# The last head pair's attention spread over sixteen gate tiles, both merge gates taken ahead of both projections, and narrower waits at three joints

## The reference, cut to what matters

```python
h = rmsnorm(x); proj = h @ w_in      # q, ff, fb, i, ga, u, v, gb, ma, mb: 1024 columns each
y_a = rmsnorm_per_head(gla_forward(q, ff, i) + gla_backward(q, fb, i)) * silu(ga)   # 8 heads
y_b = gelu(u) * mix(layernorm(gelu(v)), w_s, b_s) * silu(gb)                          # 8 groups
merged = sigmoid(ma) * (y_a @ w_proj_a) + sigmoid(mb) * (y_b @ w_proj_b)
x = x + merged @ w_out
# second block: shift, scale, gate = split(silu(c) @ ada_w + ada_b), for c and for the context's c
# h = modulate(x, ...), hc = modulate(ctx, ...), then attention mixers
```

## Time and profile before

| what | value |
|---|---|
| median of 3 runs | 1622.14 us (1621.85 to 1622.33) |
| profiled execution, own time | 1623.66 us |
| its span in the trace | 1621.8 us |
| PE busy | 1530.3 us, 94% of the span |
| DVE, ACT, POOL busy | 709.6, 654.7, 537.2 us (44, 40, 33%) |
| mean granted PE clock | 0.979 of full |
| DMA | 122.71 MB, mean 76 GB/s |

### The profile page before, as it was taken

How to read it: one execution, slowest core, us unless ns; L and a number is a source line. 1 busy time by engine, 2 the same in 40 slices (tenths; PEclk the granted TensorE clock), 3 DMA queues, 4 the chain that set the end, 5 groups by cost and what they waited for, 6 DMA issues and landing times.

```text
span 1621.8 us, 21829 instructions
## 1 busy us (share of the span) xinstructions
PE 1530.3 (94%) x8872; PEld 1240.7 (76%) x8872; DVE 709.6 (44%) x1302; ACT 654.7 (40%) x1069; POOL 537.2 (33%) x472
## 2 busy tenths in 40 slices
PE   6999999999888979999899999999998999999997
PEld 5788897888777868877688898666787876666676
DVE  3237267274386311100267412777514435444423
ACT  6233243332323422222442132777624425555652
POOL 3333332333133464444542232333522240111221
PEclk9999999999999989999999999999998999999999
DMA  5533324224111135344321120200021120000011
GB/s 183 166 107 104 104 79 130 78 79 136 47 53 52 54 103 183 129 132 154 117 78 53 53 67 21 72 21 21 13 68 53 52 65 11 11 20 27 27 53 52
DMA packets 129314, 122.71 MB, mean 76 GB/s; under 512 B 11348, under 2 KB 125152, under 8 KB 129216
## 3 DMA queue, kind: packets, MB, share of 16 engines
q1 hardware_dynamic: 128960, 121.26, 23.8%
q10 hardware_dynamic: 256, 0.07, 0.0%
HBM read 116.87 MB, written 2.10 MB: 73 GB/s over the span
## 4 chain that ended last, share of the span: by engine, by line
PE 82%; DVE 10%; ACT 4%; POOL 2%; issue 2%; DMA 1%; ACTq 0%; DVEq 0%; SPq 0%
PE ps L2012 10%; PE ps L2013 9%; PE ps L2014 9%; PE ps L2473 4%; PE ps L2494 3%; PE ps L2321 3%; PE ps L2483 3%; PE ps L2312 2%; PE ps L2219 2%; PE ps L2058 2%; PE ps L2218 2%; PE ps L2220 2%; PE ps L2086 2%; PE ps L2474 2%; PE ps L2004 2%
## 5 line engine op out<-in xcount | busy, mean ns | idle before, releaser
L1136 POOL TENSOR_TENSOR w_lo<-raw,w_hi 128x512 fp32r<-128x512 f32 x320 | 421.6, 1350 | 798.7 <-ACT w_hi L651 740.4
L2012 PE MATMUL ps<-h_hi,w_hi 128*128 128x512 f32 x632 | 255.1, 404 | 12.1 <-POOL yb_lo L1159 8.7
L2013 PE MATMUL ps<-h_lo,w_hi 128*128 128x512 f32 x632 | 248.0, 392 | 0.0
L2014 PE MATMUL ps<-h_hi,w_lo 128*128 128x512 f32 x632 | 247.6, 392 | 0.0
L651 ACT ACTIVATE w_hi<-raw 128x2048 fp32r<-128x2048 f32 (+1 forms) x77 | 145.5, 1890 | 130.2 <-PE ps L2014 32.7
L2012 PEld LDWEIGHTS ps<-h_hi,w_hi 128*128 128x128 f32 x632 | 120.4, 190 | 44.7 <-issue 18.8
L2014 PEld LDWEIGHTS ps<-h_hi,w_lo 128*128 128x128 f32 x632 | 119.7, 189 | 26.0
L2013 PEld LDWEIGHTS ps<-h_lo,w_hi 128*128 128x128 f32 x632 | 120.3, 190 | 23.2
L1901 DVE CUSTOM_DVE_ANT_0 prob_b<-ps,no_mask 128x768 f32<-128x768 f32 x64 | 61.0, 954 | 72.7 <-PE ps L2474 72.7
L1078 ACT ACTIVATE pT_b<-ps 128x512 f32<-128x512 f32 x96 | 52.1, 594 | 71.3 <-PE ps L2483 71.3
L2004 PE MATMUL ps<-w_hi,h_hi 128*128 128x256 f32 x256 | 73.7, 288 | 0.0
(11 more groups left out here) (444 smaller groups left out, 3361.0 us busy)
## 6 DMA issues: line engine op xcount, KB each, us to landing
raw<-in_w_in_dram SPq DMA_DIRECT2D x32, 1024.0 KB
raw<-in_ada_w_dram SPq DMA_DIRECT2D x24, 1024.0 KB
raw<-in_a_w_in_dram SPq DMA_DIRECT2D x10, 1024.0 KB
raw<-in_w_in_dram SPq DMA_DIRECT2D x16, 512.0 KB
raw<-in_b_w_in_dram SPq DMA_DIRECT2D x5, 1024.0 KB
raw<-in_w_proj_a_dram SPq DMA_DIRECT2D x4, 1024.0 KB
raw<-in_w_proj_b_dram SPq DMA_DIRECT2D x4, 1024.0 KB
raw<-in_w_out_dram SPq DMA_DIRECT2D x4, 1024.0 KB
```

Of the source, the lines that this page charges most:

```text
L1136: last = nc.gpsimd.tensor_tensor(w_lo[:, ph.w(s), p], raw[:, s % 2, p], w_hi[:, ph.w(s), p].bitcast(F32), ALU.subtract)
L2012: mm(ps[:, j, :], wh[:, k, c], xh[:, k, :], start=(k == 0), stop=False)
L2013: mm(ps[:, j, :], wh[:, k, c], xl[:, k, :], start=False, stop=False)
L2014: last = mm(ps[:, j, :], wl[:, k, c], xh[:, k, :], start=False, stop=(k == KT - 1))
```

## The change

Five edits:

1. `GATE_SLOT` spreads GLA slots 0 to 11 over all 16 gate tiles: tiles 2, 5, 8 and 11 have none.
2. The rounding of `y_a` leaves the gates phase. ACT does all 8 `ya_hi` at the start of the merge, behind the rounding of the second strip; POOL does `ya_lo` in two blocks of four, behind the second and the third strip's `w_lo`.
3. The merge takes ma, mb, ada, ada, pa, pb, so both gates come before both projections.
4. Waits: PE no longer waits for all of `ya_lo` and `yb_lo` ahead of the merge but tile by tile inside the first pa and pb tile. ACT's wait for `yb_lo` moves to the first mb. `ada_strip` in the heads phase waits only for the strip before the last one.
5. `c_tok` moves onto `ya_hi`'s place and its load stands behind the first w_out strip and waits only for the last pa tile.

```diff
-MERGE_STRIPS = ("ma", "pa", "ada", "ada", "mb", "pb")
+MERGE_STRIPS = ("ma", "mb", "ada", "ada", "pa", "pb")
+GATE_SLOT = (0, 1, None, 2, 3, None, 4, 5, None, 6, 7, None, 8, 9, 10, 11)
-        c_tok = at("c_tok", [P, NC, D], F32, r_vs)
+        c_tok = at("c_tok", [P, NC, D], F32, r_ya)
...
@@ SP
                     load(outs, it, s, [(k_of(raw, s % 2), w_out[:, :, (2 * it + s) * STRIP:(2 * it + s + 1) * STRIP])])
-            sp.wait_ge(s_mh, KT)
-            sp.wait_ge(s_ml, KT)
-            sp.dma_start(c_tok[:, :, :], ...).then_inc(s_in2, 16)
+                    if not (it or s):
+                        sp.wait_ge(s_proj, merge.t(merge.iters - 1, MERGE_STRIPS.index("pa")) + 2)
+                        sp.dma_start(c_tok[:, :, :], ...).then_inc(s_in2, 16)
@@ ACT, gates
-                    if tt <= 10:
-                        gla_act(g_last, tt)
+                    slot = GATE_SLOT[tt]
+                    if slot is not None:
+                        gla_act(g_last, slot)
-                    if tt >= 12:
-                        act.wait_ge(s_y, PAIRS + 1)
-                        for k in (2 * (tt - 12), 2 * (tt - 12) + 1):
-                            nc.scalar.activation(ya_hi[:, k, :], y_a[:, k, :], ACT.Copy).then_inc(s_yah, 1)
@@ ACT, merge
+                    if it == 0 and kind == "ma":
+                        act.wait_ge(s_y, PAIRS + 1)
+                        for k in range(KT):
+                            nc.scalar.activation(ya_hi[:, k, :], y_a[:, k, :], ACT.Copy).then_inc(s_yah, 1)
+                    if it == 0 and kind == "mb":
+                        act.wait_ge(s_ybl, GCH)
-            act.wait_ge(s_ybl, GCH)
@@ POOL, merge
-                for s in merge.split[1:]:
+                for x, s in enumerate(merge.split[1:]):
                     lo(merge, it, s)
+                    if it == 0 and x < 2:
+                        ya_low(*range(4 * x, 4 * x + 4))
@@ PE
-                if not (isinstance(a, int) and a < 1):
-                    pe.wait_ge(s_adaev, a)
+                free = a - 1 if ph is heads else a
+                if free > 0:
+                    pe.wait_ge(s_adaev, free)
...
-                    if tt <= 11:
-                        gla(PAIRS - 1, tt + 1)
+                    if GATE_SLOT[tt] is not None:
+                        gla(PAIRS - 1, GATE_SLOT[tt] + 1)
...
-            pe.wait_ge(s_yal, KT)
-            pe.wait_ge(s_ybl, GCH)
...
-                        project(merge, it, s, j, False, x_hi, x_lo)
+                        low = {"pa": (s_yal, 0), "pb": (s_ybl, 0)}.get(kind)
+                        project(merge, it, s, j, False, x_hi, x_lo, ready=None if it or j else low)
...
+                            if it == 0:
+                                pe.wait_ge(s_yb, GCH)
                             ada_strip(merge, it, MERGE_ADA[s, j], 7 - merge.j(MERGE_ADA[s, j]))
```

More of the change, by code:

```diff
@@ L572, in _ @@
                     load(outs, it, s, [(k_of(raw, s % 2), w_out[:, :, (2 * it + s) * STRIP:(2 * it + s + 1) * STRIP])])
-            sp.wait_ge(s_mh, KT)
-            sp.wait_ge(s_ml, KT)
-            sp.dma_start(c_tok[:, :, :], t["ctx_2"][0, :, :].rearrange("(n p) d -> p n d", p=P)).then_inc(s_in2, 16)
+                    if not (it or s):
+                        sp.wait_ge(s_proj, merge.t(merge.iters - 1, MERGE_STRIPS.index("pa")) + 2)
+                        sp.dma_start(c_tok[:, :, :], t["ctx_2"][0, :, :].rearrange("(n p) d -> p n d", p=P)).then_inc(s_in2, 16)
             sp.wait_ge(s_xt, 2 * KT)
@@ L817, in _ @@
                         nc.scalar.activation(tmp[:, 0, :], ps[:, 0, :], ACT.Square).then_inc(s_sigg, 1)
-                        gla_keys(g_last, tt)
+                        if slot is not None:
+                            gla_keys(g_last, slot)
                         hi(*((gates, (g + 1) // 2, (g + 1) % 2) if g + 1 < GCH else (merge, 0, 0)))
@@ L842, in merge_act @@
                             act.wait_ge(s_free, merge.t(it, s) + j - 1)
-                            nc.scalar.activation(tmp[:, x + j, :], ps[:, j, :], ACT.Sigmoid).then_inc(s_sigm, 1)
+                            nc.scalar.activation(tmp[:, 2 * x + j, :], ps[:, j, :], ACT.Sigmoid).then_inc(s_sigm, 1)
                         if (s, j) in MERGE_SUM:
@@ L857, in merged_hi @@
                     nc.scalar.activation(h_hi[:, k, :], merged[:, k, :], ACT.Copy).then_inc(s_mh, 1)
-            act.wait_ge(s_proj, merge.t(merge.iters - 1, merge.split[2]) + 2)
+            act.wait_ge(s_proj, merge.t(merge.iters - 1, merge.split[1]) + 2)
             merged_hi(*range(KT - 2))
@@ L1167, in _, with ya_low @@
                     split_y(g - 1)
[L1168 to L1171, removed]
             split_y(GCH - 1)
+            def ya_low(*tiles):
+                for k in tiles:
+                    pool.wait_ge(s_yah, k + 1)
+                    nc.gpsimd.tensor_tensor(ya_lo[:, k, :], y_a[:, k, :], ya_hi[:, k, :].bitcast(F32), ALU.subtract).then_inc(s_yal, 1)
             for it in range(0, merge.iters):
-                for s in merge.split[1:]:
+                for x, s in enumerate(merge.split[1:]):
                     lo(merge, it, s)
+                    if it == 0 and x < 2:
+                        ya_low(*range(4 * x, 4 * x + 4))
                 if it + 1 < merge.iters:
@@ L1519, in _ @@
                     tt = 2 * g + j
-                    gla_slot(PAIRS - 1, tt)
+                    if GATE_SLOT[tt] is not None:
+                        gla_slot(PAIRS - 1, GATE_SLOT[tt])
                     if tt == 0:
@@ L1548, in merge_dve @@
                         col = bass.ds(2 * it + j, 1)
-                        if x in (0, 2):
-                            dve.wait_ge(s_sigm, 4 * it + x + j + 1)
+                        if x < 2:
+                            dve.wait_ge(s_sigm, 4 * it + 2 * x + j + 1)
                             dve.wait_ge(s_free, merge.t(it, s) + j)
                             dve.sem_inc(s_free, 1)
-                        elif x == 1:
+                        elif x == 2:
                             dve.wait_ge(s_proj, merge.t(it, s) + j + 1)
```

## The result

| what | before | changed |
|---|---|---|
| median, first chip | 1622.24 us (1621.85 to 1622.64, 4 runs) | 1594.33 us (1591.09 to 1595.41, 4 runs) |
| ratio | | 0.9825, 95% interval 0.9808 to 0.9842 |
| profiled execution, own time | 1623.66 us | 1594.2 us |
| its span | 1621.8 us | 1592.4 us |

The forecast was 1589.5 us with a range from 1584.5 to 1599.0. The change is faster by 27.9 us by the medians and by 29.4 by the two spans, where 32.7 were forecast. The median lies in the stated range and 0.3 us above the narrower one, 1585 to 1594, that the prediction gave its own sum.

A forecast was written before the change was run, and what follows sets the result against it. PE, busy 94% of the span, was taken as the bound, its waits also lowering its clock. Heads 14.8, gates and merge 12.9 and context 5.0 sum to 32.7 us saved, giving 1589.5 us, range 1584.5 to 1599.

The forecast's parts named there:

- Heads, 14.8 us: Heads phase: the ada matmuls' four waits go, saving 3.55 us in each of three iterations and 4.15 in the first.
- Rival 2: Heads: the wait moves to DVE or a strip's load, 12 of 14.8 us stay, 1601.5 us; chance 0.05.
- Gates, wait before step 4: Gates phase: PE waits 4.5 us for DVE's doubling before GLA step 4, against 3.7 before, plus 1.4 of lower clock.
- Gates, the other waits: Gates phase: waits of 1.0 and 0.9 us for `w_lo`, 0.9 for a key copy, 3.1 before GLA step 8.
- the gain at steps 1 and 2: Early gates phase: no gain was forecast; the 2.5 us wait before GLA step 2 and its lower clock were to stay.
- The loss at step 8: Gates phase: 1.4 us lost to PE's lower clock behind the wait before GLA step 8.
- Merge, 1.85 - 1.0 = 0.85: Merge: its first tile gets 1.85 us shorter at a higher clock, less 1.0 us of waits in the first pa tile.
- Rival 3: Merge: each of its 16 `w_lo` comes late, at 3 us a strip costing 48 us, ending at 1637; chance 0.02.
- Context, 5.0 us: Context's transposes: the 5.92 us load wait goes; ACT's first copy comes 4.6 us earlier, plus 0.4 from the clock.
- Rival 1: Gates phase: DVE's doublings before GLA steps 4, 6 and 8 wait for POOL pieces, costing 8 us, 1597.5; chance 0.13.
- Rival 4: Heads, first merge tile, context: only the waits leave, clock gains shrink by 5 us, 1594.5 us; chance 0.09.
- The signs that the prediction named: Ada waits gone, merge some 27 us earlier, longest gates wait before GLA step 4, short pa wait, transposes directly behind out tile.

The follow-up runs named there:

- The experiment: Changed kernel with ACT's rounding of the third w_out strip moved behind the eight context copies to `xcT`: 1585.51 us, ratio 0.9763 to the kernel before.
- the version with early offsets: Changed kernel with DVE's eight one-time offset instructions moved from the start of gate group 1 into group 0: 1591.87 us, ratio 0.9781 to the kernel before.

## Why the prediction was right, and where it was off

- **Heads, 14.8 us: right.** The row of `k_sum` came 15.3 us earlier, and the steps next in line wait 0.22 where 0.3 was priced. Rival 2 had nothing. Alone it gave 13.2 by the medians and 13.9 by that row.
- **Gates, wait before step 4: the step that was mis-sized.** The forecast took the doubling's time behind the group's first tile from the old order, offsets included, and said 4.5 us; it measured 6.99. It took over the 2.17 us of the offsets without asking what POOL does beside them once PE, and with it the strip, comes earlier. The runs show 2.17 to 2.18 us with POOL behind, 5.3 to 6.3 with POOL beside; of the 4.15 us that they grew by, the work behind them, free of the strip, gave more than half back. (The prediction's own terms give 13.1 - 8.2 - 0.25 = 4.65 where it says 4.5, and 4.9 - 0.9 = 4.0 where the heads' first iteration says 4.15; neither changes the account.) The low clock behind the wait was right (3.78 us for the step, 3.47 in the earlier trace rows).
- **Gates, the other waits: right.** 0.47 and 0.77 for `w_lo` (1.0 and 0.9), 0.88 for the key copy (0.9), 2.83 before step 8 (3.1). Not foreseen were 1.00 us at the first doubling and 0.73 at mix(0), where PE, at full clock, now comes ahead of DVE. What these cost, the clock gave back: the last pair's first step took 2.02 us and step 2 2.16, against 2.99 and 3.55 before. The merge's start moved 588.05 - 561.87 = 26.2 us, where 26.8 (14.8 + 12.0) follow from the prediction. That these lie so close is in part luck: PE waited 16.2 us between `k_sum` and the merge where the prediction's sum leaves 12.2, and against that stand 0.5 us more from the heads and 1.5 us over this stretch that no wait explains, put down to the clock, where the prediction counted a loss of 1.4. The loss at step 8 did come (0.85 over 11.2 us behind its wait); the gain at steps 1 and 2 outweighed it.
- **Merge, 1.85 - 1.0 = 0.85: right.** Its first tile takes 5.6 us instead of 7.4, and from there to `x_again` it takes 188.9 us against 189.8. The new wait in the first pa tile is 0.46, and no later iteration waits. Rival 3 had nothing.
- **Context, 5.0 us: 4.4.** The copies stand behind ACT's rounding as said, and PE waits 2.3 us in three places. The experiment shows those waits to be the next thing to take. With the load alone the same stretch is 5.9 us shorter (54.0 us): PE's clock from these waits to that of `x_sq` was 1.00 there and 0.96 in the changed kernel.
- **Behind that, 0: a loss of 2.1 us.** The prediction had no term for later work and gave no reason. Its waits are the same, but the clock behind the `x_sq` wait was 0.58 in the changed kernel's profile and 0.83 in that of before. The windows views of those 6 us, before and then changed:

```profile
837.00:843.00 6.00, 5.17 (x37) 5.17 (x38) 2.00 (x7) 2.64 (x3) 2.09 (x2) 0.83 0.56 175
```

```profile
806.00:812.00 6.00, 5.70 (x29) 5.70 (x30) 1.47 (x6) 2.64 (x3) 2.62 (x3) 0.58 0.55 175
```

Rival 1 named the right engine pair and nearly the right place, but laid the price on the doublings. Before step 4 it was the offsets, and at step 8 the doubling kept the pace of its row. Its 8 us were 2.5. Rival 4 said 1594.5, which is nearly what was measured, but not for its reason: it took the clock's gains away at the heads, the first merge tile and the context, where they came (the first merge tile has 1.00 over 6 us, where the 8 us from 588 on had 0.76). The signs that the prediction named all came. The sum by terms was 1.2 us too high up to the first of the clock's losses (15.3 + 11.8 + 4.4 = 31.5 against 32.7), and the clock took 2.1 more. Of the 4.8 us between forecast and median, the other 1.5 come from the place of the profiled executions: that of before lay 1.4 us above its own median, that of the changed kernel on its own.

## What to carry to other kernels

A wait priced from a row of the old order holds only while the same work lies beside it: list what the neighbour engine on the shared side does at the new time, above all for a run of small two-input DVE instructions beside a GpSimd subtraction, and put one-time work where DVE waits anyway. When a change removes waits of PE, price the next late thing at each joint, as was done here to within 0.6 us at all places that the prediction named but one; two waits, of 1.00 and 0.73 us, it didn't name. Expect 2 to 4 us either way from the clock behind waits that stay. Compare several profiles of one kernel before a clock difference is called the program's.

## What the runs showed of the hardware

- Eight DVE instructions of 128x128 elements with two SBUF inputs take 2.17 us alone and 5.29 to 6.32 beside POOL's subtraction, which keeps 1.33 us a piece there (5.30 to 5.31 us for four). Beside the doubling of the version with early offsets POOL's four pieces took 6.03 us.
- After the same wait of 1.7 us PE's granted clock fell to the lower level, 1.2 GHz, in all 13 profiles. In five it was still at 1.00 for over 2 us from the start of `x_sq` and lacked 1.7 us of full speed in all; in the others it fell within the first 1 us or so and lacked 3.4 or 5.1. Two executions of one kernel had 1.7 and 5.1, and their rests differ by 3.6 us. After waits of 2.53 to 2.54 us GLA step 2 takes between 2.16 and 3.55 us, from profile to profile.
- The changed kernel gained 27.9, 33.4 and 33.1 us on three occasions. The kernel before was the one that differed (1622.24, 1627.32, 1625.97), more than the first ratio's interval tells: the three are 0.9825, 0.9786 and 0.9796.
